# Down weights of the fixed expert blocks: requests moved from SyncE's queue to ScalarE's

## The chip, the cores and the metric

The kernel runs on one core of one Trainium2 chip, as one program. The metric is the device time of that program in microseconds (us). Times come as the median of several runs, and one further execution was recorded by the hardware profiler; all rows below are from that execution.

## The reference

One inference step of a trunk of two layers over 640 tokens (512 latent and 128 context) of width 1024, in 32-bit floats. Each layer is a modulated norm, four mixers side by side (convolution, Hyena, Fourier, attention) behind one input and one output projection, a gated residual, a second norm, and a mixture of experts. Only the last part matters here:

```python
def hier_moe(h, rc_w, rc_b, rf_w, rf_b, e_gate, e_up, e_down):
    ...
    def run(args):
        tok, e = args
        xb = t[tok]
        return (jax.nn.silu(xb @ e_gate[e]) * (xb @ e_up[e])) @ e_down[e]

    yb = lax.map(run, (slot_tok.reshape(nb, MOE_BLOCK), blk_e))
```

There are 32 experts a layer. A router gives each token two of them. `e_gate[e]` and `e_up[e]` are 1024 x 256, `e_down[e]` is 256 x 1024, so each of the three is 1 MB, and every expert's weights are read once a layer whatever the router says.

## The kernel before

The expert stage of a layer runs in blocks of at most 64 rows (`BR`) of one expert. The first 28 blocks (`NSTAT`) are fixed: block n is expert n. What is left (experts 28 to 31, and experts with more than 64 rows) runs in an overflow loop of two blocks a turn whose experts are read from a table. The five engines each have their own order of instructions and meet by semaphores.

One block goes like this. GpSimd gathers the block's rows from DRAM into `xg` (line 852). TensorE turns them (`rows_in`, line 1346), ScalarE copies them out to `xe` (line 1713). TensorE multiplies with gate and up (`gate_up`, line 1355, 32 matmuls). ScalarE takes the SiLU (line 1720), VectorE multiplies by the up half (line 2228), TensorE turns the product (`hidden_in`, line 1362), VectorE copies it (line 2230), TensorE multiplies with down (`down`, line 1370, 8 matmuls). ScalarE copies the result to `ye` (line 1727), GpSimd scatters it to `Y_dram` (line 857) and then starts the gather three blocks on. TensorE turns the rows of block n + 1 between `gate_up` and `hidden_in` of block n. In layer 0, TensorE, ScalarE, VectorE and GpSimd also make layer 1's Hyena filters in between, and ScalarE stores two spectra of 1280 KB (`filter_store`, line 1510).

The weights lie in places of 16 KB a partition, `units`: a pair for gate and up of one block, one for down. Layer 0 has three pairs and two places for down, layer 1 four pairs and three places. A place is free when the product that read it is done. In this kernel SyncE (SP) asks for all of them on its one queue, in the order of the products that free the places: after `gate_up` of block n (semaphore `g_mm`) gate and up of block n + 3 (layer 0) or n + 4 (layer 1), lines 682 and 683, and after `down` of block n (`y_mm`) down of block n + 2 or n + 3, line 687. The first downs of a layer (two or three) are asked for ahead of that loop, those of the overflow loop inside it, both by SP.

ScalarE waits for `y_mm` of a block too, since it copies the product's result; `over_clear` tells in layer 1 that the semaphores of the overflow loop have been set back.

Of the kernel before, what the change touches and what calls it, by code (L numbers as in the profile page):

```python
# [26 lines left out]
NG, EPG, NE, FE = 4, 8, 32, 256  # L27
TOPK = 2
SLOTS = 2
# [8 lines left out]
NSTAT = NE - 2 * SLOTS  # L38
# [61 lines left out]
def trunk(nc, io, out):  # L100
    ctx = ExitStack()
    with ctx:
        def sem(name):
            return ctx.enter_context(nc.semaphore(name))
# [127 lines left out]
        units = [ring[:, i, :] for i in range(6)] + [v.rearrange("p q t -> p (q t)") for v in (inv_s, mix_s, fwd_s)] \  # L232
            + [hflat[:, i * UNIT:(i + 1) * UNIT] for i in range(2)]
        gu_units = [[(0, 1), (3, 4), (6, 7)], [(0, 1), (3, 4), (6, 7), (9, 10)]]
        dn_units = [[2, 5], [2, 5, 8]]
# [185 lines left out]
        g_mm = sem("g_mm")  # L421
# [4 lines left out]
        y_mm = sem("y_mm")  # L426
# [3 lines left out]
        d_wd = [sem(f"d_wd{s}") for s in range(SLOTS)]  # L430
# [16 lines left out]
        over_clear = sem("over_clear")  # L447
# [29 lines left out]
        def nth(l, s, n):  # L477
            return per_layer[s.num] * l + n
# [15 lines left out]
        def dn_slot(l, n):  # L494
            return n % len(dn_units[l])

        def gu_sem(l, n):
            return w_full[gu_slot(l, n)]

        def dn_sem(l, n):  # L500
            return (wd_full + a_full[:1])[dn_slot(l, n)]
# [56 lines left out]
        def _(sp):  # L558
# [66 lines left out]
            for l in range(DEPTH):  # L625
# [53 lines left out]
                def gate_up_in(n, e, done):  # L679

                    g, u_ = gu_units[l][gu_slot(l, n)]
                    sp.dma_start(units[g], gate[e]).then_inc(done, 16)
                    sp.dma_start(units[u_], up[e]).then_inc(done, 16)

                def down_in(n, e, done):

                    sp.dma_start(units[dn_units[l][dn_slot(l, n)]], down[e]).then_inc(done, 16)

                def gate_up_next(n):

                    gate_up_in(n, l * NE + n, gu_sem(l, n) if n < NSTAT else d_wg[n % SLOTS])

                def down_next(n):

                    down_in(n, l * NE + n, dn_sem(l, n) if n < NSTAT else d_wd[n % SLOTS])
# [3 lines left out]
                down = io["exp_down"].rearrange("l e (p k) f -> (l e) p (k f)", k=2)  # L699
                ahead_g, ahead_d = len(gu_units[l]), len(dn_units[l])  # L700
# [11 lines left out]
                if l:  # L712
                    sp.wait_ge(hs_mm, nth(l, hs_mm, 10))
                    gate_up_next(3)
                for n in range(NSTAT + SLOTS - ahead_d):
                    if n + ahead_d == NSTAT and l > 0:
                        sp.wait_ge(over_clear, l)
                    if n + ahead_g < NSTAT + SLOTS:
                        sp.wait_ge(g_mm, nth(l, g_mm, n + 1))
                        gate_up_next(n + ahead_g)  # L720
                    sp.wait_ge(y_mm, nth(l, y_mm, n + 1))
                    down_next(n + ahead_d)
                sp.wait_ge(ro_tab, l + 1)
                turns = sp.value_load(nturn[0:1, 0:1], min_val=SLOTS, max_val=(NBLK - NSTAT) // SLOTS)
                with sp.Fori(1, turns) as j:
                    for s in range(SLOTS):
                        e = sp.value_load(ebi[0:1, bass.ds(j * SLOTS + (s + NSTAT), 1)], min_val=0, max_val=NE - 1)
# [720 lines left out]
        def _(act):  # L1448
# [31 lines left out]
            def filter_sine(l, n):  # L1480

                act.wait_ge(hy_phase, 2 * l + n + 1)
                A((h1, h2)[n][l][0:FFN, :], fa_[l][0:FFN, :], ACT.Sin).then_inc(hy_sine, 1)

            def filter_abs(l, o, t):

                n = 10 * l + 5 * o + t
                act.wait_ge(hy_eo, n + 1)
                if n >= 2:
                    act.wait_ge(hy_sum, 7 * ((n - 2) // NT) + (n - 2) % NT + 1)  # L1490
                A(fabs[l][:, t % 2, :, :], ftime[l][:, t % 2, :, :], ACT.Abs).then_inc(hy_abs, 1)

            def filter_even(l, o, f):

                fo = 2 * l + o
                act.wait_ge(hy_k, 3 * fo + f + 1)
                if fo:
                    act.wait_ge(hy_kd, 2 * (fo - 1) + f + 1)
                A(ek[l][:, f, :, :], ps[:, FB, :].rearrange("p (q c) -> p q c", q=2), ACT.Copy).then_inc(hy_es, 1)

            def filter_store(l, o):

                fo = 2 * l + o
                if fo:
                    act.wait_ge(k_out, 16 * fo)
                act.wait_ge(hy_k, 3 * fo + 3)
                A(knew[:, :, 4, :], ps[:, FB, :].rearrange("p (q c) -> p q c", q=2), ACT.Copy).then_inc(hy_ke, 1)
                act.wait_ge(hy_ke, fo + 1)
                act.wait_ge(hy_kd, 2 * (fo + 1))
                act.dma_start(K_dram[fo], knew.rearrange("p q t c -> p (q t c)")).then_inc(k_out, 16)  # L1510
# [44 lines left out]
            for l in range(DEPTH):  # L1555
# [153 lines left out]
                act.wait_ge(hs_st[1], nth(l + 1, hs_st[1], 0))  # L1709
                act.wait_ge(ro_tab, l + 1)  # L1710

                def rows_out(s):
                    return A(xe[:, s, :, :], ps[:, 0, :].rearrange("p (k t) -> p k t", k=4), ACT.Copy)  # L1713

                act.wait_ge(xt_mm, nth(l, xt_mm, 1))
                rows_out(0).then_inc(xe_ok, 1)
                for n in range(NSTAT):
                    s = n % SLOTS
                    act.wait_ge(g_mm, nth(l, g_mm, n + 1))
                    A(sg[BR:P, s, :], ps[0:BR, 1, 0:FE], ACT.Silu).then_inc(sg_ok, 1)  # L1720
                    if n + 1 < NSTAT:
                        act.wait_ge(xt_mm, nth(l, xt_mm, n + 2))
                        rows_out(1 - s).then_inc(xe_ok, 1)
                    act.wait_ge(y_mm, nth(l, y_mm, n + 1))
                    if n >= SLOTS:
                        act.wait_ge(y_out[s], nth(l, y_out[s], 16 * (n // SLOTS)))
                    A(ye[:, s, :], ps[:, 3, :], ACT.Copy).then_inc(ye_ok, 1)  # L1727
                    if l + 1 < DEPTH:
                        if n == 3:
                            filter_sine(l + 1, 0)  # L1730
                        elif n == 5:
                            filter_sine(l + 1, 1)
                        elif 6 <= n < 6 + NT:
                            filter_abs(l + 1, 0, n - 6)
                        elif n in (12, 13):
                            filter_even(l + 1, 0, n - 12)
                        elif n == 14:
                            filter_store(l + 1, 0)
                        elif 15 <= n < 15 + NT:
                            filter_abs(l + 1, 1, n - 15)  # L1740
                        elif n in (20, 21):
                            filter_even(l + 1, 1, n - 20)
                        elif n == 22:
                            filter_store(l + 1, 1)
# [3 lines left out]
                turns = act.value_load(nturn[0:1, 0:1], min_val=SLOTS, max_val=(NBLK - NSTAT) // SLOTS)  # L1748
                act.wait_ge(d_xt, 1)
                rows_out(0).then_inc(d_xe, 1)  # L1750
                with act.Fori(0, turns) as j:
                    for s in range(SLOTS):
# [566 lines left out]
```

## Time and profile before

| | us |
|---|---|
| median of 3 runs | 1568.39 |
| lowest, highest | 1562.25, 1570.11 |
| the profiled execution | 1564.04 |
| its span, first to last instruction | 1562.2 |
| busy in the span: TensorE matmuls | 1264.4 |
| VectorE | 540.9 |
| ScalarE | 380.6 |
| GpSimd | 259.1 |

The span is the profiled execution without its first and last moments. Busy time of an engine is summed over the span; it says how much an engine does, not whether it is in the way. Transfers run on 16 DMA engines that all queues share: SP's queue moved 324.35 MB, GpSimd's 22.03 MB, ScalarE's 11.08 MB. Their share in a stretch is the mean of the 16 engines' busy time. The granted clock of TensorE (PEclk) is given as a share of full speed, 1.00 being 2.4 GHz and 0.50 being 1.2 GHz. A row that names a line of the source as `SPq`, `ACTq` or `POOL DMA_INDIRECT` is the issue of a transfer; "to landing" is the time from the issue to the completion.

### The profile page before, as it was taken

To read this page: it belongs to the slowest core of one execution; us is meant where nothing else is said; L and a number is where in the kernel's file an instruction comes from. 1 tells how busy PE (TensorE), PEld (TensorE's weight loads), DVE (VectorE), ACT (ScalarE), POOL (GpSimd) and SP (SyncE) were. 2 spreads that over 40 slices of the span, in tenths; PEclk is the share of its full clock that TensorE was granted. 3 is DMA by queue.
4 is the path that set the end of the run, shared out by engine and by line. 5 is a ranking of instruction groups with operands and counts; after the bars stand their busy time and mean duration, and the time that the engine had idled before them with its cause. 6 is when DMAs were issued, how large, how long until landed. Compare 5 with 4: busy or idle time off the path is not lost.

```text
span 1562.2 us, 16661 instructions
## 1 busy us (share of the span) xinstructions
PE 1264.4 (81%) x6542; PEld 733.9 (47%) x6542; DVE 540.9 (35%) x1136; ACT 380.6 (24%) x741; POOL 259.1 (17%) x273
## 2 busy tenths in 40 slices
PE   3899998877998698999884799897699678888870
PEld 1456474445344354655442466544555444444430
DVE  3326456354114332121003367554622510000006
ACT  3410115310224122122124311432014212211123
POOL 4210110002000134242231008100100022222220
PEclk9899999988998699999897799999799689998995
DMA  9737320053647599999897220102120669999965
GB/s 353 258 135 276 135 78 27 32 198 137 218 170 268 195 415 419 409 419 397 349 410 283 99 81 21 58 27 88 46 96 27 283 247 419 417 418 419 406 242 205
DMA packets 73520, 358.45 MB, mean 229 GB/s; under 512 B 13197, under 2 KB 22027, under 8 KB 37736
## 3 DMA queue, kind: packets, MB, share of 16 engines
q1 hardware_dynamic: 58012, 324.35, 53.6%
q0 software_dynamic: 12704, 22.03, 3.9%
q10 hardware_dynamic: 2732, 11.08, 1.8%
q8 instruction: 49, 0.80, 0.2%
q14 instruction: 23, 0.19, 0.0%
HBM read 340.32 MB, written 31.23 MB: 238 GB/s over the span
## 4 chain that ended last, share of the span: by engine, by line
PE 64%; DMA 13%; DVE 11%; ACT 6%; issue 5%; POOL 1%; ACTq 0%; SPq 0%; POOLq 0%; DVEq 0%
PE ps L1355 10%; PE ps L1303 9%; PE ps L1370 7%; PE ps L1150 5%; DMA work<-h_scratch,tabs 4%; PE ps L1060 4%; PE ps L1111 3%; PE ps L921 3%; PE ps L1081 2%; PE ps L1260 2%; DMA mix_s<-in_exp_up 2%; PE ps L1362 1%; DMA ring<-in_ada_w 1%; PE ps L974 1%; PE ps L1157 1%
## 5 line engine op out<-in xcount | busy, mean ns | idle before, releaser
L1355 PE MATMUL ps<-ring,work 128*64 128x256 f32 x1312 | 158.9, 397 | 3.9 <-ACT work L1713 3.1
L1370 PE MATMUL ps<-ring,work 128*64 128x512 f32 x456 | 120.9, 653 | 33.7 <-DVE work L2230 18.2
L1303 PE MATMUL ps<-ring,yT 128*128 128x512 f32 x320 | 143.8, 599 | 2.0 <-DVE yT L2091 2.0
L1355 PEld LDWEIGHTS ps<-ring,work 128*64 128x64 f32 x1312 | 103.8, 145 | 72.4 <-issue 30.9
L2228 DVE TENSOR_TENSOR work<-work,ps 64x256 f32<-64x256 f32 x56 | 23.8, 424 | 325.0 <-ACT work L1720 325.0
L857 POOL DMA_INDIRECT y_scratch<-work,tabs x56 | 57.5, 1028 | 322.2 <-ACT work L1727 322.2
L1968 DVE SCALAR_TENSOR_TENSOR work<-work,prmT 128x655 f32<-128x655 f32 x120 | 97.7, 895 | 0.0
L1303 PEld LDWEIGHTS ps<-ring,yT 128*128 128x128 f32 x320 | 59.0, 191 | 74.7 <-issue 72.5
L852 POOL DMA_INDIRECT work<-h_scratch,tabs x60 | 61.7, 1028 | 173.2 <-DVE tabs L2216 147.4
L1150 PE MATMUL ps<-hT,ring 128*128 128x512 f32 x192 | 88.6, 604 | 1.1 <-DVE ring L1985 1.1
L1355 PE MATMUL ps<-inv_s,work 128*64 128x256 f32 x320 | 72.4, 379 | 1.7 <-DMA mix_s<-in_exp_up 1.7
L1727 ACT ACTIVATE work<-ps 128x512 f32<-128x512 f32 x56 | 33.4, 597 | 163.2 <-PE ps L1370 163.2
L1060 PE MATMUL ps<-hT,ring 128*128 128x512 f32 x128 | 70.1, 631 | 3.4 <-POOL hT L818 1.9
L1355 PE MATMUL ps<-mix_s,work 128*64 128x256 f32 x320 | 72.4, 379 | 0.0
L921 PE MATMUL ps<-ring,c_act 128*32 128x512 f32 x384 | 53.7, 633 | 19.6 <-DMA ring<-in_ada_w 17.6
L1370 PEld LDWEIGHTS ps<-ring,work 128*64 128x64 f32 x456 | 30.2, 141 | 75.8 <-issue 47.0
L1260 PE MATMUL ps<-inv_s,hT 128*128 128x256 f32 x128 | 42.2, 493 | 28.0 <-POOL hT L839 17.6
L1713 ACT ACTIVATE work<-ps 128x512 f32<-128x512 f32 x70 | 41.8, 597 | 94.6 <-PE ps L1346 94.6
L1346 PE MATMUL ps<-sq,work 128*128 128x128 f32 x280 | 46.1, 288 | 22.3 <-DMA work<-h_scratch,tabs 16.7
L826 POOL TENSOR_TENSOR yT<-yT 128x512 f32<-128x512 f32 x4 | 32.3, 8068 | 166.2 <-ACT yT L1581 166.2
L1720 ACT ACTIVATE work<-ps 64x256 f32<-64x256 f32 x56 | 21.0, 375 | 157.6 <-PE ps L1355 157.6
L1355 PEld LDWEIGHTS ps<-inv_s,work 128*64 128x64 f32 x320 | 43.7, 137 | 32.1 <-issue 13.6
(378 smaller groups left out, 1961.2 us busy)
## 6 DMA issues: line engine op xcount, KB each, us to landing
ring<-in_exp_down SPq DMA_DIRECT2D x57, 1024.0 KB, 14.1
ring<-in_ada_w SPq DMA_DIRECT2D x48, 1024.0 KB, 4.9
ring<-in_exp_gate SPq DMA_DIRECT2D x41, 1024.0 KB, 11.6
ring<-in_exp_up SPq DMA_DIRECT2D x41, 1024.0 KB, 15.4
inv_s<-in_exp_gate SPq DMA_DIRECT2D x20, 1024.0 KB, 10.6
mix_s<-in_exp_up SPq DMA_DIRECT2D x20, 1024.0 KB, 15.3
ring<-in_w_in SPq DMA_DIRECT2D x16, 1024.0 KB, 8.2
fwd_s<-in_exp_down SPq DMA_DIRECT2D x11, 1024.0 KB, 19.7
```

What stands on the lines that cost most here:

```text
L852: pool.indirect_dma_start(xg[:, s, :], None, H_half, bass.IndirectOffsetOnAxis(ap=rows.bitcast(U32), axis=0), bounds_check=2 * T - 1, oob_ ...
L857: pool.indirect_dma_start(Y_half, bass.IndirectOffsetOnAxis(ap=rows.bitcast(U32), axis=0), ye[:, s, :], None, bounds_check=2 * T * TOPK - ...
L921: last = mm(ps[32 * g:32 * g + 32, 5, :], c_act[:, k, :], w[:, 512 * g:512 * g + 512], start=(k == 0), stop=(k == KC - 1))
L1060: mm(ps[:, m, :], lhs, hT[:, k, 0:LS], start=(k == 0), stop=(k == KC - 1))
L1111: mm(ps[:, bank, :], lhs, hT[:, k, 0:LS], start=(k == 0), stop=(k == KC - 1))
L1150: last = mm(ps[:, 7, :], wh[m // 2][:, k, m % 2 * P:(m % 2 + 1) * P], hT[:, k, 0:LS], start=(k == 0), stop=(k == KC - 1))
L1260: mm(ps[:, 6 + c, e * CH:(e + 1) * CH], yspec[:, q, 2 * e + f, c * P:(c + 1) * P], inv_s[:, 2 * f + q, e * CH:(e + 1) * CH], start=(q + f ...
L1303: last = mm(ps[:, (4, 6, 7, 0)[n % 4], :], yT[:, k, t * P:(t + 1) * P], wo[k // 2][:, k % 2, h * HALF:(h + 1) * HALF], start=(k == 0), sto ...
L1346: last = tr(ps[:, 0, k * P:(k + 1) * P], xg[:, s, k * P:(k + 1) * P], ident)
L1355: last = mm(ps[BR * q:BR * q + BR, 1, 0:FE], xe[:, s, kb, BR * h:BR * h + BR], w[q][:, k, :], start=(k == 0), stop=(k == KC - 1))
L1370: last = mm(ps[BR * h:BR * h + BR, 3, :], he[:, s, k, :], wd[:, k, HALF * h:HALF * h + HALF], start=(k == 0), stop=(k == 1))
L1968: V.scalar_tensor_tensor(out=acc[:, c, :], in0=glu[:, c, j:j + CONV], scalar=prmT[:, c, j:j + 1], in1=acc[:, c, :], op0=ALU.mult, op1=ALU. ...
```

## The change

SP's loop over the fixed blocks keeps the requests for gate and up and loses those for down, with the waits for `y_mm`. ScalarE asks for down of block n + 2 (layer 0) or n + 3 (layer 1) itself, right after its own wait for `y_mm` of block n and ahead of the wait for the scatter and the copy of that block. Sizes, places and semaphores of the transfers stay. The downs asked for ahead of the loop and those of the overflow loop stay with SP; the downs of the two blocks with which the overflow loop begins are asked for by ScalarE now.

```diff
-                for n in range(NSTAT + SLOTS - ahead_d):
-                    if n + ahead_d == NSTAT and l > 0:
+                for n in range(NSTAT + SLOTS - ahead_g):
+                    if n + ahead_g == NSTAT and l > 0:
                         sp.wait_ge(over_clear, l)
-                    if n + ahead_g < NSTAT + SLOTS:
-                        sp.wait_ge(g_mm, nth(l, g_mm, n + 1))
-                        gate_up_next(n + ahead_g)
-                    sp.wait_ge(y_mm, nth(l, y_mm, n + 1))
-                    down_next(n + ahead_d)
+                    sp.wait_ge(g_mm, nth(l, g_mm, n + 1))
+                    gate_up_next(n + ahead_g)
...
+                down = io["exp_down"].rearrange("l e (p k) f -> (l e) p (k f)", k=2)
+                ahead = len(dn_units[l])
+
+                def down_next(n):
+
+                    if n == NSTAT and l > 0:
+                        act.wait_ge(over_clear, l)
+                    act.dma_start(units[dn_units[l][dn_slot(l, n)]], down[l * NE + n]) \
+                        .then_inc(dn_sem(l, n) if n < NSTAT else d_wd[n % SLOTS], 16)
+
...
                     act.wait_ge(y_mm, nth(l, y_mm, n + 1))
+                    if n + ahead < NSTAT + SLOTS:
+                        down_next(n + ahead)
                     if n >= SLOTS:
                         act.wait_ge(y_out[s], nth(l, y_out[s], 16 * (n // SLOTS)))
                     A(ye[:, s, :], ps[:, 3, :], ACT.Copy).then_inc(ye_ok, 1)
```

## Rows read from the trace of the kernel before

**Rows 1.** Busy by stretch: us, engines, granted clock, DMA share, GB/s.
```profile
528.00:768.00 240.00, 215.47 (x1407) 124.43 (x1406) 52.03 (x125) 53.98 (x102) 70.00 (x69) 0.97 0.98 398
1259.00:1485.00 226.00, 194.90 (x1284) 108.59 (x1284) 20.03 (x56) 44.13 (x84) 55.91 (x55) 0.93 0.98 401
1350.00:1485.00 135.00, 113.88 (x716) 63.89 (x712) 11.45 (x32) 23.92 (x46) 32.18 (x32) 0.90 1.01 413
770.00:780.00 10.00, 8.41 (x50) 4.80 (x52) 0.72 (x2) 1.57 (x3) 2.18 (x4) 0.83 0.57 204
```

**Rows 2.** Transfers, 1268 to 1475 us, in 40 slices: GB/s of all queues.
```profile
GB/s 407 374 415 429 416 416 422 417 424 411 423 418 417 418 416 413 422 419 418 413 418 417 422 412 420 420 417 422 416 422 418 419 419 416 418 415 420 423 416 416
```

**Rows 3.** Chain of waits, layer 1's first blocks: start, us, what.
```profile
1268.45 3.48 PE ps L1355 x32
...
1275.61 3.48 PE ps L1355 x32
```

**Rows 4.** The scatters of layer 0's, then layer 1's fixed blocks: first, last start.
```profile
L857 POOL DMA_INDIRECT y_scratch<-work,tabs x28: 1005/1014/1460, 539.5 to 769.8; - x28
...
L857 POOL DMA_INDIRECT y_scratch<-work,tabs x28: 1007/1013/1023, 1269.9 to 1486.6; - x28
```

**Rows 5.** Timeline of TensorE, late in layer 1: start, us, what, idle time before it.
```profile
1403.69 0.44 PE L1362 MATMUL ps<-sq,work 64*128 64x64 f32 x2 [0.35 <-DVE work L2228]
1405.89 3.19 PE L1370 MATMUL ps<-ring,work 128*64 128x512 f32 x8 [1.76 <-issue]
1408.80 4.17 PE L1355 MATMUL ps<-hT,work 128*64 128x256 f32 x32
...
1414.73 1.94 PE L1370 MATMUL ps<-ring,work 128*64 128x512 f32 x8 [0.38 <-DVE work L2230]
```

**Rows 6.** One down, one up request, their landings; then all layer 1's L687 landings.
```profile
L687 SPq DMA_DIRECT2D ring<-in_exp_down x1: 328/328/328, 1382.4 to 1382.4; - x1
...
DMA to landing us min/median/max: 23.4/23.4/23.4
...
L683 SPq DMA_DIRECT2D hT<-in_exp_up x1: 433/433/433, 1379.1 to 1379.1; - x1
...
DMA to landing us min/median/max: 24.0/24.0/24.0
...
DMA to landing us min/median/max: 7.3/21.9/23.9
```

**Rows 7.** Layer 0's downs, then its gathers, by line, with landings.
```profile
L687 SPq DMA_DIRECT2D ring<-in_exp_down x28: 327/328/328, 538.1 to 768.4; - x28
...
DMA to landing us min/median/max: 7.6/13.4/15.4
...
L852 POOL DMA_INDIRECT work<-h_scratch,tabs x28: 997/1026/1066, 528.8 to 761.3; - x28
...
DMA to landing us min/median/max: 3.3/7.2/10.9
```

**Rows 8.** ScalarE's store with landing; next scatter's and gather's landings; TensorE behind.
```profile
L1510 ACTq DMA_DIRECT2D k_scratch<-yT x1: 352/352/352, 657.5 to 657.5; - x1
...
DMA to landing us min/median/max: 11.8/11.8/11.8
...
DMA to landing us min/median/max: 9.3/9.3/9.3
...
DMA to landing us min/median/max: 10.9/10.9/10.9
...
670.04 0.66 PE L1346 MATMUL ps<-sq,work 128*128 128x128 f32 x4 [1.50 <-DMA work<-h_scratch,tabs]
```

**Rows 9.** Timeline of ScalarE and GpSimd behind layer 0's first down product.
```profile
538.12 0.60 ACT L1727 ACTIVATE work<-ps 128x512 f32<-128x512 f32 x1 [2.54 <-PE ps L1370]
...
540.86 1.03 POOL L852 DMA_INDIRECT work<-h_scratch,tabs  x1 [0.30 <-issue]
```

**Rows 10.** Timeline of TensorE, down product of layer 0's last fixed block.
```profile
764.80 3.58 PE L1370 MATMUL ps<-ring,work 128*64 128x512 f32 x8 [1.39 <-issue]
```

## The prediction

> **What bounds the kernel now.** I read the page first: its chain of waits lies mostly on TensorE, with transfers second, so I went to the two stretches that the change touches, the fixed expert blocks of the two layers (about 528 to 768 us and 1259 to 1485 us), with busy time by stretch [rows 1]. There TensorE is busy for 215 of 240 us and 195 of 226 us, and the 16 DMA engines have a share of 0.98 of both, 1.01 in the last 135 us of the second: they never rest. The rates say the same: in slices of 5 us they stand at 411 to 424 GB/s almost without exception, 429 the highest [rows 2]. So both stretches run at the transfers' pace for most of their length, with TensorE close behind.
>
> How close? Where nothing is late one gate/up product begins 7.16 us after the one before (1275.61 less 1268.45) [rows 3]. The scatters give the real pace: 28 of them in each layer, so 27 blocks in 216.7 us or 8.03 us each in layer 1, and in 230.3 us or 8.53 us each in layer 0, where TensorE also builds the next layer's filters [rows 4].
>
> Next I looked for what TensorE waits for in the late part of layer 1 [rows 5]. The hidden transpose at 1403.69 is over at 1404.13; the down product waits until 1405.89 and takes 3.19 us, the next one, unhindered, 1.94 us. The late one runs at a lower granted clock: the stretch has 0.90, against 0.93 for the whole stage [rows 1]. What it waited for is its weights: asked for at 1382.4, landed 23.4 us later, at 1405.8 [rows 6]. The up weights of the following block were asked for at 1379.1 and landed at 1403.1, 5.7 us before their product at 1408.80 began [rows 5, 6]. That is the present balance: SP's one queue carries gate and up of a later block ahead of down of an earlier one, so down comes just in time or late (median 13.4 us to landing in layer 0) [rows 7], and gate/up has about 5 us in hand.
>
> **The change part by part.** The numbers below are for one profiled execution of 1564.04 us, which is 4.35 us under the median of the runs shown, 1568.39; half a per cent, 7.8 us, is about what a measurement of this kernel can tell from no change, the three runs before being 7.9 us apart.
>
> (a) *SP loses the requests.* Layer 0 asked for 28 downs in its loop, layer 1 for 27. SP only waits and issues here, and its requests for gate/up still follow the same gate/up products. 0 us.
>
> (b) *ScalarE gains them.* A transfer request on ScalarE's queue takes 0.35 us [rows 8], so 55 of them are 19 us of its time, in stretches where it is busy for 54 of 240 and 44 of 226 us [rows 1]. The request stands in front of the copy of the block's output. Behind that copy is the scatter on GpSimd, behind the scatter the gather of the rows three blocks on; all of it moves 0.35 us later. ScalarE's next work is the SiLU after the next gate/up product, 3.5 us later [rows 3], and the request (0.35) and the copy (0.60) [rows 9] are through before it. Without that cover it would be 55 x 0.35 = 19 us; I take 0, apart from the gather, in (d).
>
> (c) *Down no longer queues behind gate/up.* The trace has no load on ScalarE's queue in this stretch, but a store of 1280 KB does run there while SP's queue is full: 11.8 us [rows 8]. By size a 1024 KB down takes some 9.4 us (an estimate, 11.8 x 0.8); bounds 7.3, the shortest landing of SP's downs in layer 1, and 11.8. All are under the 13.4 and 21.9 us medians [rows 6, 7], and under two block periods less the product (2 x 7.16 - 1.94 = 12.4). So the down waits should go. But bytes are neither fewer nor faster: with the engines at 1.01, what comes sooner makes gate/up come later, by one to two downs of 1 MB, 2.5 to 5 us at 418 GB/s, against the 5 us in hand. TensorE then waits a little at the gate/up product instead, and the stage ends when the same bytes are through. I take 0 for the part bound by transfers. Bounds: +4 (two layers, 2 us each) if gate/up overshoots its reserve; -10 if layer 0, whose stretch runs at 398 against 411 to 424 GB/s (3% of 240 us is 7 us) [rows 1, 2], also fills its lean slices.
>
> One place is not bound by bytes: the last fixed block of layer 0. Its down product waits 1.39 us and then takes 3.58 us instead of 1.94 [rows 10], and just after it the engines' share falls to 0.57 [rows 1], so nothing further is late. That is 1.39 - 0.38 (the usual gap) + 1.64 = 2.65 us saved. Layer 1 ends without such a wait. Sum of (c): -2.7.
>
> (d) *The gather shares the engines with one more queue.* Its median in layer 0 is 7.2 us [rows 7]. With the store beside it the gather took 10.9 and the scatter ahead of it 9.3; TensorE waited 1.50 us for the rows at 670.04 [rows 8]. 7.2 and 10.9 are the ends. A down is smaller than the store, and is asked for 3.1 us ahead of the gather (2.74 + 0.35, below), the store only 1.6 us (657.5, and 670.0 less 10.9), so more of it is gone when the gather starts: I take the middle, 8.5 to 9. What that means is read from the loop through the gather. From the output copy to the gather's start 2.74 us [rows 9], then the landing L, then the rows' transpose, 0.66 [rows 8], the hidden transpose, 0.44, the usual gap, 0.38, and the down product, 1.94 [rows 5], 3.4 us together. This loop spans two blocks, so it allows a period of (2.74 + 0.35 + L + 3.4)/2: 6.8 us for L = 7.2 (covered by the 7.16), 7.6 for 8.75, 8.7 for 10.9. At 7.6 the early blocks of layer 1 lose their pace of 7.16, but the transfers catch them later anyway (8.03 on average); I take +1 for both layers together, with 0 and +23 as bounds (below).
>
> Sum: 0 + 0 - 2.7 + 1 = about -2, so 1562 for the profiled execution and **1566.5 us** against the median.
>
> Two rules of the Trainium skill bear on this, and both speak against a gain. DMA: Bandwidth & Descriptors, "Issuing engines are not separate DMA queues", says that transfers of all issuing engines end on the same 16 engines and that issuing from several saves only the issue time; by it alone (c) would be 0 and the sum +1. The trace agrees for the rate (418 GB/s with the queues that run now). The same page, "Queues, rings and completion order", says that an engine takes turns between its queues packet by packet; an even turn would give the store half of 418 GB/s, by estimate 6.3 us, and a down 5, gone before the gather is under way, with (d) 0 and the sum -3. The trace differs: the store took 11.8 us [rows 8], and the sum above goes by that.
>
> **The rivals.**
> *The gather becomes the bound (slower).* A wait at the rows takes the place of that at the down product. For it: it waits in TensorE's order ahead of the hidden transpose, the store shows 10.9, and a wait is often followed by a slower product (3.19 against 1.94, which would add 1.25/2 us to a period). Against it: when TensorE slows, the queues empty and the gather gets shorter. It decides where the loop's period passes 8.03 us: 2 x 8.03 - 6.5 = 9.6 us for L, or 8.3 with the slow product each time. Layer 0's blocks with extra TensorE work have slack of their own. At L = 10.9 throughout, layer 1 would lose 27 x 0.67 = 18 us and layer 0 27 x 0.17 = 5 us: +23. At a middle L of 10 with some slow products: 27 x 0.4 = 11, and some 3 in layer 0: +14, 1582.
>
> *The transfers gain from a second queue (faster).* If 16 engines fed from two queues ran at the best slice, 429 instead of 418 GB/s [rows 2], the two stages of 466 us would shrink by 2.6%: -12 us, 1556. For it only that TensorE could use them: 8.03 and 8.53 against 7.16. Against it: the share is already 1.01, and a store of 11.8 us is no sign of spare rate [rows 1, 8].
>
> *Hidden anyway (no change).* Down lands no earlier than before, since ScalarE's queue gets a small part: 11.8 us for the store is near layer 0's 13.4. Then the time is 1568; it lies with my forecast.
>
> **How the numbers follow.** Forecast, with hidden anyway: 0.58. Gather bound: 0.28; the price is near the half per cent, and its condition (L of 9.6) lies between the rows' ends. Second queue faster, or the lean slices of layer 0 filled together with the tail: 0.14. The likeliest case has 1558 to 1575 as its own range (-10 to +4 around the median, and the spread of the runs). To leave out no more than 2 in 10 it reaches to both rivals' prices: 1556 to 1582. Faster than 1560.5: 0.14; within half a per cent: 0.58; slower than 1576.2: 0.28.
>
> **What would show it.** Right: 55 requests of some 0.35 us on ScalarE's queue at the down's line; down landing in 8 to 11 us in both layers; no down product of over 3 us after a wait in layer 1's late part; gate/up landing longer than before; the scatters of a layer still 27 x 8.0 and 27 x 8.5 us apart from first to last; the share still about 1.0. Wrong: gathers of 10 us and over with waits at the rows' transposes and the engines' share under 0.95 (gather bound), or a rate over 425 GB/s with shorter stages (second queue).

## The result, and the profile after

The changed kernel takes 1580.98 us (median of 4 runs, 1575.51 to 1586.99), the kernel before 1567.1 us in the runs beside it: a ratio of 1.0097, 95% interval 1.0071 to 1.0122. It is slower by some 15 us, where no change was forecast. The profiled execution has a span of 1577.6 us, 15.4 us more than before.

Busy time by stretch in the changed kernel, the two stages and a piece late in layer 1; columns as in [rows 1]:

```profile
528.00:778.00 250.00, 223.56 (x1410) 123.17 (x1410) 52.07 (x125) 54.03 (x102) 69.35 (x69) 0.94 0.96 383
1270.00:1502.00 232.00, 192.88 (x1287) 101.70 (x1285) 20.06 (x56) 45.28 (x85) 56.10 (x55) 0.94 0.97 394
1362.00:1502.00 140.00, 115.93 (x774) 60.80 (x768) 12.18 (x34) 26.51 (x51) 34.69 (x34) 0.94 0.99 406
```

Against [rows 1] the share of the DMA engines has sunk a little, 0.98 to 0.96 and 0.97, and from 1.01 to 0.99 late in layer 1: in places the transfers now wait for somebody. The scatters, layer 0 and then layer 1, give the pace, as [rows 4] did:

```profile
L854 POOL DMA_INDIRECT y_scratch<-work,tabs x28: 1007/1012/1080, 541.4 to 779.9; - x28
...
L854 POOL DMA_INDIRECT y_scratch<-work,tabs x28: 1011/1017/1024, 1282.4 to 1502.3; - x28
```

27 blocks in 238.5 us instead of 230.3, and in 219.9 instead of 216.7: 8.2 and 3.2 us. The rest of the 15.4 us lies outside the changed stages (1.9 us ahead of the first, some 2 between them) and is within what two executions differ by.

What does TensorE wait for? First the kernel before, two lines for layer 0 and two for layer 1 (us in total, times, longest), then the changed one, a line for each; "issue" at L1370 is a wait in which the profile names nobody, and [rows 5, 6] show for one of them that it was for the weights:

```profile
PE ps L1370 <- issue: 6.3, 4, 1.8
...
PE ps L1346 <- DMA work<-h_scratch,tabs: 3.2, 3, 1.5
...
PE ps L1370 <- issue: 7.1, 4, 1.8
PE ps L1346 <- DMA work<-h_scratch,tabs: 2.3, 3, 0.9
```

```profile
PE ps L1343 <- DMA work<-h_scratch,tabs: 11.9, 8, 2.7
...
PE ps L1343 <- DMA work<-h_scratch,tabs: 22.2, 18, 3.0
```

These waits of the down product, 13.4 us, are gone. In their place stands the wait of the rows' transpose for the gather: 34.1 us, after 5.5. Layer 0's downs and gathers, then layer 1's, with the times from issue to landing:

```profile
L1716 ACTq DMA_DIRECT2D ring<-in_exp_down x28: 334/334/358, 539.6 to 778.2; - x28
...
DMA to landing us min/median/max: 7.3/8.5/9.6
...
L849 POOL DMA_INDIRECT work<-h_scratch,tabs x28: 1000/1029/1066, 529.9 to 774.1; - x28
...
DMA to landing us min/median/max: 3.4/8.3/11.6
...
DMA to landing us min/median/max: 9.2/9.9/10.8
...
L849 POOL DMA_INDIRECT work<-h_scratch,tabs x28: 1007/1024/1031, 1271.3 to 1496.8; - x28
...
DMA to landing us min/median/max: 2.9/8.6/10.5
```

Down lands in 8.5 and 9.9 us (13.4 and 21.9 before [rows 6, 7]), the gather in 8.3 and 8.6 (before, 7.2 in layer 0 [rows 7] and 7.3 in layer 1). And the chain of waits in layer 1 of the changed kernel (start, us, what) is, where TensorE waits for the rows, a loop that returns to the gather every two blocks:

```profile
1316.26 9.26 DMA work<-h_scratch,tabs
...
1325.57 0.66 PE ps L1343 x4
1326.23 0.44 PE ps L1359 x2
...
1326.69 0.30 DVE work L2239
...
1327.04 3.33 PE ps L1367 x8
...
1330.39 0.33 ACTq L1716
...
1330.77 0.61 ACT work L1736
...
1332.17 1.02 POOL y_scratch L854
...
1333.49 7.95 DMA work<-h_scratch,tabs
```

Gather, rows' transpose, hidden transpose, down product (3.33 us, slow), the new request, the output's copy, the scatter, the next gather: 17.2 us for two blocks, 8.6 each, with the request for down as one link of it. This is the first rival of the prediction.

### The profile page after: what moved, and what is told of

Same layout as the page of the kernel before. It is cut to its first block, busy times and chain, and to the rows that moved or that the text cites. A ratio compares the mean times of both kernels' runs of the same rounds, so it can differ in the third digit from the quotient of the medians.

```text
span 1577.6 us, 16611 instructions
## 1 busy us (share of the span) xinstructions
PE 1271.2 (81%) x6542; PEld 725.0 (46%) x6542; DVE 541.2 (34%) x1136; ACT 380.9 (24%) x741; POOL 258.8 (16%) x273
## 4 chain that ended last, share of the span: by engine, by line
PE 58%; DMA 18%; DVE 11%; ACT 6%; issue 5%; POOL 2%; ACTq 1%; POOLq 0%; SPq 0%; DVEq 0%
DMA work<-h_scratch,tabs 12%; PE ps L1300 9%; PE ps L1367 6%; PE ps L1352 6%; PE ps L1147 5%; PE ps L1057 4%; PE ps L918 3%; PE ps L1108 3%; PE ps L1078 2%; PE ps L1257 2%; DMA ring<-in_ada_w 2%; DMA mix_s<-in_exp_up 1%; PE ps L1343 1%; PE ps L971 1%; PE ps L1154 1%
## 5 line engine op out<-in xcount | busy, mean ns | idle before, releaser
L1367 PE MATMUL ps<-ring,work 128*64 128x512 f32 x456 | 124.4, 671 | 21.9 <-DVE work L2239 18.0
L1352 PEld LDWEIGHTS ps<-ring,work 128*64 128x64 f32 x1312 | 99.0, 145 | 77.5 <-issue 34.4
L1343 PEld LDWEIGHTS ps<-sq,work 128*128 128x128 f32 x280 | 31.3, 145 | 80.3 <-DMA work<-h_scratch,tabs 48.5
L1367 PEld LDWEIGHTS ps<-ring,work 128*64 128x64 f32 x456 | 29.9, 146 | 67.7 <-issue 37.9
```

The lines of the kernel that those rows point to most:

```text
L1343: last = tr(ps[:, 0, k * P:(k + 1) * P], xg[:, s, k * P:(k + 1) * P], ident)
L1352: last = mm(ps[BR * q:BR * q + BR, 1, 0:FE], xe[:, s, kb, BR * h:BR * h + BR], w[q][:, k, :], start=(k == 0), stop=(k == KC - 1))
L1367: last = mm(ps[BR * h:BR * h + BR, 3, :], he[:, s, k, :], wd[:, k, HALF * h:HALF * h + HALF], start=(k == 0), stop=(k == 1))
```

## The experiments

The theory (G): the gather sets the pace. ScalarE's queue makes it land later, and the request ahead of the output's copy makes it start later. Rivals: the order of the weights, down ahead of gate/up (O); the second queue moves fewer bytes per us (Q); the late copy by itself (L). All ratios are to runs of the kernel before on the same chip, with 95% intervals.

### The request behind the copy

```diff
-                    if n + ahead < NSTAT + SLOTS:
-                        down_next(n + ahead)
...
                     A(ye[:, s, :], ps[:, 3, :], ACT.Copy).then_inc(ye_ok, 1)
+                    if n + ahead < NSTAT + SLOTS:
+                        down_next(n + ahead)
```

> The changed kernel with ScalarE's request for down moved behind the copy of the block's output. Gather theory: TensorE waits for the gathered rows, which start 0.35 us later and land 1.3 us later than before. Taking away the 0.35 us shortens the loop through the gather by 0.18 us a block; with some 26 waits in the two layers that is 3 to 6 us off 1581: 1575 to 1578. Rival (order: down goes ahead of gate/up, and gate/up is what is late) and rival (two hardware queues move fewer bytes): no change, 1579 to 1583.

Measured: 1568.36 us, ratio 1.0025 (1.0005 to 1.0046). Three quarters of the loss, 0.72% or 11 us, hung on the 0.35 us for which the copy waited. The direction is G's, the size twice what I had written. The gather still lands in 8.1 and 8.8 us (medians of the two layers), so the later landing is still there, and 0.25% remains with it.

### The gather ahead of the scatter

The gather for block n + 3 needs only that the rows of block n + 1 are turned, which is before the down product of block n.

```diff
+                gather_behind(0)
                 for n in range(NSTAT):
                     s = n % SLOTS
-                    pool.wait_ge(xt_mm, nth(l, xt_mm, n + 1))
-                    pool.wait_ge(xg_in[s], nth(l, xg_in[s], 16 * (n // SLOTS + 1)))
-                    if n + SLOTS == NSTAT and l > 0:
-                        pool.wait_ge(over_clear, l)
-                    gather_rows(s, tabs[:, 0, n + SLOTS:n + SLOTS + 1], xg_in[s] if n + SLOTS < NSTAT else d_xg[s])
+                    if n + 1 < NSTAT:
+                        gather_behind(n + 1)
                     pool.wait_ge(ye_ok, nth(l, ye_ok, n + 1))
```

(`gather_behind(n)` holds the lines taken out.) In the changed kernel:

> The changed kernel with each gather started ahead of the scatter of the block before instead of behind it, so some 4 us earlier (as soon as its place is free). Gather theory: the waits at the rows' transposes, 34 us in the changed kernel's two stages, go, and the time falls by 12 to 20 us to 1561 to 1569; whatever the second queue costs beyond the gather stays in it. Rivals (order of the weights, fewer bytes per us): waits move to the gate/up products, 1577 to 1583.

Measured: 1568.48 us, ratio 1.0012 (0.999 to 1.0034). With the gather off the loop the loss is gone; O and Q expected it to stay. What TensorE waits for in layer 1 of this kernel:

```profile
PE ps L1358 <- DMA ring<-in_exp_up: 7.8, 8, 1.4
PE ps L1358 <- DMA mix_s<-in_exp_up: 7.7, 5, 2.0
PE ps L1358 <- DMA hT<-in_exp_up: 6.3, 5, 1.5
```

The gate/up product for its up weights: the wait that the prediction put behind the vanished down waits, and at nearly the same time for the stage, 218.4 us for 27 blocks against 216.7. The same edit in the kernel before:

> The kernel before with the same early gather. Gather theory: before, TensorE waited only 5.5 us for the rows, most of it hidden by the transfers' pace: 1560 to 1567, at most 0.4 per cent faster. If the gather was the bound of the kernel before too, 1550 to 1558.

Measured: 1565.92 us, ratio 1.0002 (0.9984 to 1.002). The kernel before had nothing to gain from it.

### One queue, down first

```diff
-                    if n + ahead_g < NSTAT + SLOTS:
-                        sp.wait_ge(g_mm, nth(l, g_mm, n + 1))
-                        gate_up_next(n + ahead_g)
                     sp.wait_ge(y_mm, nth(l, y_mm, n + 1))
                     down_next(n + ahead_d)
+                    if n + ahead_g < NSTAT + SLOTS:
+                        gate_up_next(n + ahead_g)
```

> The kernel before, all requests on SyncE's queue, with down of a block asked for ahead of the gate and up that used to precede it (both behind the down product). One queue, other order. Gather theory: no second queue, so gathers land in about 7.2 us as before and the time is 1563 to 1570. Order theory: down ahead of gate/up costs what the change cost, 1576 to 1585. Two-queue theory: as before, 1563 to 1570.

Measured: 1568.32 us, ratio 1.0015 (0.9998 to 1.0031). Here too TensorE's largest waits for a transfer in layer 1 are those for up weights (20.6 us in all), so the order does move the wait, and it costs 0.3% at most, a third of the loss. O falls.

### One layer at a time

In the layer left out, SyncE's loop is that of before and ScalarE asks for nothing (`if l == 0`, then `if l == 1`).

> The change in layer 0 alone; layer 1 asks for everything on SyncE's queue as before. Gather theory, from the scatters of the changed kernel: layer 0's blocks lost 8.2 us, layer 1's 3.1 us; here 1572 to 1576 against 1565. If the loss belongs to the late, transfer-bound part of layer 1: 1564 to 1567.

> The change in layer 1 alone. Gather theory: the transfers' pace gives back most of what the gather costs, so 2 to 5 us over the kernel before: 1566 to 1570. If a second queue moves fewer bytes per us: layer 1, the stage nearest to the transfers' pace, would carry half the loss or more, 1572 and over.

Measured: layer 0 alone 1571.97 us, ratio 1.0044 (1.0018 to 1.0069); layer 1 alone 1570.92 us, 1.0037 (1.0015 to 1.0059). Together 0.81%, within the intervals of 0.97%. In each run the gather lands late only in the layer that has requests on ScalarE's queue: with layer 0 changed, medians of 8.1 us in layer 0 and 7.4 in layer 1; with layer 1 changed, 7.3 and 8.5. Layer 1 costs somewhat more than I expected from the single profile (3.2 us of scatters); Q had put half the loss or more there, and this run does not exclude it, the early gather does.

### The delay alone, and twice

The delay without a request is one more ScalarE copy of 0.38 us that changes no value, ahead of the output's copy:

```diff
+                    A(sg[BR:P, s, :], sg[BR:P, s, :], ACT.Copy)
                     if n >= SLOTS:
                         act.wait_ge(y_out[s], nth(l, y_out[s], 16 * (n // SLOTS)))
                     A(ye[:, s, :], ps[:, 3, :], ACT.Copy).then_inc(ye_ok, 1)
```

In the kernel before:

> The kernel before with one more copy of 0.38 us on ScalarE (the SiLU's result onto itself, 64 x 256, which changes no value) ahead of the copy of the block's output; all requests on SyncE's queue. Gather theory: the gather starts 0.38 us later but lands in 7.2 us as before, so the loop through it is 6.9 us a block, under 7.16: 1563 to 1568. If the late copy alone is the cost: 1573 to 1580.

Measured: 1567.23 us, ratio 1.0008 (0.9994 to 1.0021). At most 0.2%: L falls. In the changed kernel, on top of the request:

> The changed kernel with the same 0.38 us copy besides the request, so twice the delay ahead of the output's copy. Gather theory: the loop is already the bound in many blocks, so each 0.38 us of delay costs about what the request's 0.35 us cost (some 10 us between the changed kernel and the one with the copy first): 1586 to 1594. If what matters is the second queue and not the gather's start: 1579 to 1583.

Measured: 1586.8 us, ratio 1.0144 (1.0123 to 1.0166), 0.47% or 7 us more than the change. And with the request behind the copy, so that only the copy's delay is left:

> The changed kernel with the request for down behind the copy of the output, as in the run that got most of the loss back, but with the 0.38 us copy (values unchanged) ahead of that copy: the gather starts as late as in the changed kernel, while down is asked for some 1 us later than there. Gather theory: the loss is back, 1576 to 1583. If the copy-first run was faster because down's load came later and met the scatter differently: 1565 to 1571.

Measured: 1579.82 us, ratio 1.0097 (1.0069 to 1.0126), the change's own figure to the last place. When down is asked for makes no difference; when the gather starts does.

### More load on ScalarE's queue

ScalarE also asks for the up weights, behind the SiLU:

```diff
                     A(sg[BR:P, s, :], ps[0:BR, 1, 0:FE], ACT.Silu).then_inc(sg_ok, 1)
+                    if n + ahead_g < NSTAT + SLOTS:
+                        up_next(n + ahead_g)
```

> The changed kernel with the up weights too on ScalarE's queue, asked for behind the SiLU; SyncE's queue keeps gate. Two of three MB of each block come by ScalarE's queue, which is then busy through the gather's whole time; ScalarE's delay ahead of the output's copy stays one request. Gather theory: gathers land in 9.5 to 10.5 us instead of 8.5, the loop is 0.5 to 1 us a block longer where it binds: 1588 to 1605. If the delay ahead of the copy is the whole loss and the second queue's load counts for nothing: 1579 to 1583.

Measured: 1598.93 us, ratio 1.0218 (1.0192 to 1.0244). The gathers of layer 0 and layer 1:

```profile
DMA to landing us min/median/max: 2.8/9.0/11.9
...
DMA to landing us min/median/max: 2.9/9.6/11.1
```

With the delay ahead of the copy unchanged, 0.8 and 1.1 us more of landing (8.2 and 8.5 in the same stretches of the changed kernel) go with 1.2% more time; TensorE's waits for a transfer here are all for the rows. In layer 0 the gather was a little quicker than expected.

### Both costs taken away, and fewer bytes

> The changed kernel with the request behind the copy and the early gather together: nothing left of either cost. Theory of the transfers' pace: the same bytes in the same stages, 1562 to 1568, no better than before. If the change has a gain of its own that the gather hid, here it shows: 1553 to 1560.

Measured: 1564.46 us, ratio 0.9994 (0.9976 to 1.0011). The change has no gain of its own that the gather hid. Is it the transfers that hold it there? The same kernel with less to load in layer 1 (the second half of each down that ScalarE asks for is left out there, so that layer's output is not the right one):

```diff
-                    act.dma_start(units[dn_units[l][dn_slot(l, n)]], down[l * NE + n]) \
+                    cut = D if l + 1 == DEPTH else UNIT
+                    act.dma_start(units[dn_units[l][dn_slot(l, n)]][:, 0:cut], down[l * NE + n][:, 0:cut]) \
```

> The changed kernel with the request behind the copy and the early gather, and in layer 1's blocks only the first 512 KB of each down that ScalarE asks for is loaded (the second half of a down's rows keeps what its place held before, so layer 1's expert output differs); instructions and routing stay. Some 15 per cent fewer bytes in that stage. If the transfers set its pace, as the prediction had it: from 8.1 us a block towards 7.2 to 7.4, 27 times 0.7 to 0.9, so 1541 to 1549. If something else keeps the stage at 8.0 us a block now that gather and down waits are gone: 1560 to 1567.

Measured: 1539.19 us, ratio 0.9838 (0.9811 to 0.9864), a little more gained than expected. Its scatters in layer 1:

```profile
L854 POOL DMA_INDIRECT y_scratch<-work,tabs x28: 1007/1013/1022, 1267.1 to 1460.3; - x28
```

193.2 us for 27 blocks, 7.16 us each: TensorE's own pace [rows 3]. At full bytes the same kernel took 218.8 us. So the stage of layer 1 does run at the transfers' pace in this kernel. The kernel before and the other versions whose gather keeps up with it take 216.7 to 218.4 us there, which fits, though bytes were taken out of this one alone.

## Why the prediction was wrong

**Right: (a), (b) as far as ScalarE goes, and (c).** The 55 requests take 0.33 us each; down lands in 8.5 and 9.9 us, where 9.4 was estimated; its waits are gone; what replaces them, once the gather is out of the way, is a wait for up weights at nearly the same stage time; nothing was to be gained, and fewer bytes gave 25 us at once. The tail of layer 0 came as written. Its last fixed block in the changed kernel, against [rows 10]:

```profile
776.19 1.94 PE L1367 MATMUL ps<-ring,work 128*64 128x512 f32 x8 [0.38 <-DVE work L2239]
```

**The step that failed is (d)**, "the transfers catch them later anyway [...]; I take +1". Its landing was right, with some luck, as the middle between two rows: L of 8.5 to 9 taken, 8.3 and 8.6 measured. Its price was not: some 15 us and more (the tail gave 2.6 back), and nothing of it clear of the noise is left once the gather is off the loop (1.0012 and 0.9994). Two things were wrong in it.

First the loop. I worked out 7.6 us a block with a down product of 1.94 us, and kept the slower product after a wait for the rival. But a wait for the rows can bring it too. Timeline of TensorE in layer 0 of the changed kernel:

```profile
701.82 1.11 PE L1343 MATMUL ps<-sq,work 128*128 128x128 f32 x4 [1.51 <-DMA work<-h_scratch,tabs]
702.86 0.50 PE L1359 MATMUL ps<-sq,work 64*128 64x64 f32 x2
703.75 3.68 PE L1367 MATMUL ps<-ring,work 128*64 128x512 f32 x8 [0.39 <-DVE work L2239]
```

Transpose 1.11 instead of 0.66, product 3.68 instead of 1.94. What that is worth is read from the first to the last scatter of layer 0 and of layer 1, columns as in [rows 1], before and then after:

```profile
539.50:769.80 230.30, 205.86 (x1348) 118.97 (x1344) 51.31 (x123) 51.12 (x98) 69.01 (x68) 0.98 1.01 409
1269.90:1486.60 216.70, 185.14 (x1227) 103.24 (x1224) 19.32 (x54) 41.78 (x80) 54.94 (x55) 0.94 1.00 412
```

```profile
541.40:779.90 238.50, 211.86 (x1344) 116.55 (x1340) 51.35 (x123) 51.18 (x98) 68.35 (x68) 0.95 0.99 395
1282.40:1502.30 219.90, 182.11 (x1223) 96.00 (x1220) 19.34 (x54) 41.83 (x80) 55.13 (x55) 0.95 1.00 408
```

In layer 0 the same work keeps TensorE busy for 6.0 us more, at a lower granted clock, and idle for 2.2 us more: in this execution most of the 8.2 us are slower products. In layer 1 it is busy for 3.0 us less and idle for 6.2 us more: there the loss is waiting, and 6 of its down products are slow (over 2.5 us) where 8 were before.

Second the cover. 8.03 us was an average of quick early blocks and of late ones at the transfers' pace, so a loop under 8.03 us can still cost time. The twelfth scatter of layer 1, before and after:

```profile
1349.66 1.01 POOL L857 DMA_INDIRECT y_scratch<-work,tabs  x1 [5.12 <-ACT work L1727]
...
1370.34 1.02 POOL L854 DMA_INDIRECT y_scratch<-work,tabs  x1 [4.81 <-ACT work L1736]
```

The first 11 blocks took 79.8 us before and 87.9 after: 8.0 us a block, where I had worked out 7.6 (two of their products were slow, not each one), and 7.25 before. The other 16 took 136.9 and 131.9. So the transfers did catch up, by 5 of the 8 us, and not by all of it. In layer 0 nothing is caught up where TensorE has the filters to make: there it is busy almost without a break, the intervals between scatters are the same in both kernels in several blocks (10.24, 8.50 and 7.16 us), and I read from this that time lost ahead of them stays lost. From 690 to 730 us, before and then after:

```profile
690.00:730.00 40.00, 38.17 (x257) 24.73 (x254) 7.69 (x19) 8.77 (x18) 13.53 (x14) 1.00 1.00 398
```

```profile
690.00:730.00 40.00, 36.96 (x220) 21.49 (x218) 7.61 (x18) 8.22 (x16) 12.78 (x13) 0.91 0.92 346
```

The engines' share falls to 0.92, the granted clock to 0.91. In some of these blocks GpSimd's own filter work stands between scatter and gather, in both kernels (2.42 us from one start to the other instead of 1.32), which the loop of (d) left out.

The experiments fit a reserve that two small costs use up. Before, the loop took (2.74 + 7.2 + 3.4) = 13.3 us of the 14.3 us of two blocks, 1.0 us of reserve:

| ahead of the copy | one queue | down on ScalarE's queue | up and down there |
|---|---|---|---|
| nothing | 1 | 1.0025 | |
| 0.33 to 0.38 us | 1.0008 | 1.0097 and 1.0097 | 1.0218 |
| 0.7 us | | 1.0144 | |

The delay alone fits into the reserve; the later landing alone (0.9 to 1.6 us) uses it up; from there each 0.35 us is paid in every loop. 27 loops of two blocks in both layers make 9.5 us; measured were 11 (0.72%) and 7 (0.47%). That sum of costs that only count beyond a reserve is my reading of the table (TensorE waited for rows 26 times in these stages); that neither cost makes the loss by itself is shown.

**The rivals.** The gather as the bound came true, at a landing lower than the 9.6 us that I gave it with unhindered products; its chance of 0.28 leaned on that figure. The sizes that I had set as its signs were too coarse: gathers of 10 us and a share under 0.95 were not reached (8.6 and 0.96). The second queue brought no higher rate. Layer 1 of the changed kernel, 1280 to 1490 us, in 40 slices:

```profile
GB/s 417 356 426 425 415 422 420 421 421 417 408 424 403 419 418 418 420 415 421 418 417 414 418 419 419 424 416 418 421 417 418 419 400 416 412 418 421 373 415 421
DMA packets 14866, 87.14 MB, mean 415 GB/s; under 512 B 3253, under 2 KB 3253, under 8 KB 5201
```

The best slice is 426, where [rows 2] has 429. Of the two rules of the Trainium skill, DMA: Bandwidth & Descriptors, "Issuing engines are not separate DMA queues" is borne out in that spreading brought no bytes (1.0012 and 0.9994 with the gather out of the way); the saved issue time that it grants cost time here, since it was moved to an engine whose next instruction was waited for. Even turns, as I made of "Queues, rings and completion order", would have a 1 MB down land in some 5 us (an estimate from that page); 8.5 and 9.9 were measured.

Open: why a load on ScalarE's queue makes a gather land 0.9 to 1.6 us later was not taken apart. It seems to hang on when the two meet: with the early gather and the same load it landed in 7.7 and 7.5 us. And a profile of one execution doesn't settle how the loss is split between the layers: that of the run with the request behind the copy and the copy's delay has 1.2 us of it in layer 0 and 7.5 in layer 1.

## What to carry to other kernels

Before a request is moved to another engine, ask which instruction it will stand in front of and follow that one's result to the next loop: 0.35 us ahead of a copy cost 11 us here, behind it nothing of that. A loop that is "covered" by another bound is covered only by its reserve, and small costs add up to it: price them together, with the slower products that follow some waits, and stretch by stretch instead of against an average. A stage at the transfers' pace gained nothing here from another order of the same bytes.

## What the runs showed that I had not expected

After the wait of 1.51 us at the rows at 701.82 the next products ran at half speed: 3.68 against 1.94 us for the down product, at a granted clock of 0.50, the lower level of 1.2 GHz:

```profile
704.00:706.00 2.00, 2.00 (x6) 0.51 (x6) 1.73 (x5) 0.00 (x0) 0.00 (x0) 0.50 1.01 420
```

Not every such wait does that. In the kernel before, the product behind the wait of 1.50 us of [rows 8] ran at full speed:

```profile
671.46 1.94 PE L1370 MATMUL ps<-ring,work 128*64 128x512 f32 x8 [0.39 <-DVE work L2230]
```

And a second queue beside a full first one got a small part of the rate: 1 MB in 9.9 us, some 106 GB/s of 415, in layer 1. The gathers paid for it, 7.2 and 7.3 us before, 8.3 and 8.6 after, and 9.0 and 9.6 with two thirds of the weights on ScalarE's queue.
